# Index scores summed over the heads by TensorE with diagonal weights, instead of by VectorE

## What is computed

```python
sc = jnp.einsum('bqhd,bsd->bqhs', qi, ki)
idx_score = jnp.einsum('bqhs,bqh->bqs', jax.nn.relu(sc), wib)
idx_score = jnp.where(causal[None], idx_score, NEG)
_, sel = lax.top_k(idx_score, k_top)          # k_top = 64
...                                           # softmax attention over the selected keys
```

## Time and profile before

| | |
|---|---|
| median of 3 runs | 1553.19 us (1549.77 to 1553.95) |
| profiled execution | 1555.47 us, of which the span from first to last instruction is 1553.7 us |
| TensorE busy | 1497.1 us, 96% of the span |
| VectorE busy | 1063.1 us, 68% |
| ScalarE busy | 778.6 us, 50% |
| mean granted TensorE clock | 0.990 |

### The profile page before, as it was taken

The page is one execution under the profiler, slowest core; times in us unless marked ns, Lnnn a source line. Parts: engine busy times, 40 slices in busy tenths (PEclk is TensorE's granted clock), DMA queues, the critical chain, the costliest instruction groups (busy, mean ns, idle before and its releaser), DMA issues.

```text
span 1553.7 us, 21682 instructions
## 1 busy us (share of the span) xinstructions
PE 1497.1 (96%) x8433; PEld 1264.5 (81%) x8433; DVE 1063.1 (68%) x1713; ACT 778.6 (50%) x1162; POOL 123.3 (8%) x98
## 2 busy tenths in 40 slices
PE   8989999999899999999999999999999999999997
PEld 5767888888777888878877988888788779888886
DVE  7767588667866787676345566878864455677777
ACT  4564444434464444433655344666545653446563
POOL 0130000000220000011022000000010320000000
PEclk9999999999999999999999999999999999999999
DMA  7624655655334755654614745556536147355551
GB/s 257 199 99 139 201 192 190 211 179 192 117 120 155 242 192 188 219 173 135 190 59 151 252 134 171 185 189 217 175 122 193 53 150 258 125 168 185 189 189 67
DMA packets 184429, 265.03 MB, mean 171 GB/s; under 512 B 7368, under 2 KB 139398, under 8 KB 184200
## 3 DMA queue, kind: packets, MB, share of 16 engines
q1 hardware_dynamic: 178712, 258.38, 50.1%
q10 hardware_dynamic: 5616, 5.26, 1.0%
HBM read 258.38 MB, written 5.24 MB: 170 GB/s over the span
## 4 chain that ended last, share of the span: by engine, by line
PE 77%; DVE 13%; ACT 5%; issue 2%; DVEq 2%; POOL 1%; ACTq 0%; POOLq 0%; DMA 0%; SPq 0%
PE psw L815 18%; PE psw L814 8%; PE psw L742 8%; PE psw L744 7%; PE psw L743 7%; DVE wlo L1736 5%; PE psa L742 4%; PE psa L744 4%; PE psa L743 4%; PE psa L874 3%; PE psa L876 3%; PE psa L927 2%; PE psw L898 2%; ACT sy L1452 1%; PE psa L944 1%
## 5 line engine op out<-in xcount | busy, mean ns | idle before, releaser
L1736 DVE TENSOR_TENSOR wlo<-raw,whi 128x2048 fp32r<-128x2048 f32 (+3 forms) x199 | 449.9, 2266 | 125.0 <-ACT whi L1348 124.5
L815 PE MATMUL psw<-xboth,whi 128*128 128x512 f32 x1344 | 464.8, 396 | 1.2 <-DVE wlo L1736 1.2
L1348 ACT ACTIVATE whi<-raw 128x2048 fp32r<-128x2048 f32 (+3 forms) x199 | 375.2, 1886 | 175.8 <-PE psw L744 91.3
L814 PE MATMUL psw<-xboth,wlo 128*128 128x256 f32 x1176 | 327.9, 279 | 0.0
L815 PEld LDWEIGHTS psw<-xboth,whi 128*128 128x128 f32 x1344 | 242.7, 188 | 49.1 <-DVE wlo L1736 2.3
L814 PEld LDWEIGHTS psw<-xboth,wlo 128*128 128x128 f32 x1176 | 221.7, 189 | 7.5
L742 PE MATMUL psw<-whi,xboth 128*128 128x512 f32 (+3 forms) x472 | 182.1, 386 | 5.3 <-DVE wlo L1736 5.3
L744 PE MATMUL psw<-whi,xboth 128*128 128x512 f32 (+3 forms) x472 | 178.9, 379 | 0.0
L743 PE MATMUL psw<-wlo,xboth 128*128 128x512 f32 (+3 forms) x472 | 178.9, 379 | 0.0
L1410 ACT ACTIVATE r<-psw 128x512 f32<-128x512 f32 x88 | 52.5, 596 | 174.6 <-PE psw L815 164.0
L742 PE MATMUL psa<-whi,rr 128*128 128x512 f32 x352 | 137.5, 391 | 1.4 <-DVE rr L2366 1.4
(11 more groups left out here) (290 smaller groups left out, 2210.1 us busy)
## 6 DMA issues: line engine op xcount, KB each, us to landing
raw<-in_w_gu SPq DMA_DIRECT2D x44, 1024.0 KB, 5.1
raw<-in_ffn_w_up SPq DMA_DIRECT2D x42, 1024.0 KB, 5.1
raw<-in_w_down SPq DMA_DIRECT2D x22, 1024.0 KB, 4.9
raw<-in_ffn_w_down SPq DMA_DIRECT2D x22, 1024.0 KB, 4.9
raw<-in_w_in SPq DMA_DIRECT2D x20, 1024.0 KB, 5.3
raw<-in_xa_wkv SPq DMA_DIRECT2D x16, 1024.0 KB, 5.3
raw<-in_w_o SPq DMA_DIRECT2D x8, 1024.0 KB, 5.1
raw<-in_w_out SPq DMA_DIRECT2D x8, 1024.0 KB, 5.2
```

The costliest lines, as they stand in the source:

```text
L814: pe.matmul(bank[:, 0:S], wl[:, k, cols], xhi[:, k, :], start=False, stop=False)
L815: ins = pe.matmul(bank.rearrange("p (i s) -> p i s", i=2), wh[:, k, cols], xboth[:, :, k, :], start=k == 0, stop=k == KD - 1)
L1348: nc.scalar.activation(tile_flat("hi", i), tile_flat("raw", i), ACT.Copy).then_inc(hi_ready, 1)
L1736: v.tensor_tensor(tile_flat("lo", i), tile_flat("raw", i), tile_flat("hi", i).bitcast(F32), ALU.subtract).then_inc(lo_ready, 1)
```

## The change

For each tile, ScalarE makes eight diagonal matrices `diag` (the identity scaled, row by row, by the query's weight for a head), and TensorE multiplies each with the head's relu'd scores and accumulates the eight products in one PSUM bank (`index_sum`, now TensorE's). VectorE only adds the mask while it copies that sum out (`index_out`). Scores, relu and head transposes move in all three programs, two PSUM banks of late heads change (`head_banks`), and the top-k rounds are spread anew: four of tile 0 ahead of the last rope, two behind it, two in step 0 of attention, and tile 1's eight over steps 1 to 5 as 2, 1, 2, 1 and 2.

```diff
+TOP_STEPS = {0: (0, 6, 8), 1: (1, 0, 2), 2: (1, 2, 3), 3: (1, 3, 5), 4: (1, 5, 6), 5: (1, 6, 8)}
+        diag = cblocks[:, 0:2048].rearrange("p (t h s) -> p t h s", t=NT, h=H)
+        isum_banks = [psw[:, 0, :], psa[:, 2, :]]
+        head_banks = [(psa, 0), (psa, 1), (psw, 2), (psw, 1), (psw, 3), (psa, 0), (psa, 1), (psa, 3)]
...
+                def index_sum(t):                                   # TensorE
+                    nk = (t + 1) * P
+                    pe.wait_ge(relu_done, NT * l + t + 1)
+                    pe.wait_ge(diag_ready, NT * l + t + 1)
+                    for h in range(H):
+                        ins = pe.matmul(isum_banks[t][:, 0:nk], diag[:, t, h, :], relu[:, h, 0:nk],
+                                        start=h == 0, stop=h == H - 1)
+                    ins.then_inc(isum_done, 1)
+                def second_scores():
+                    pe.wait_ge(proj_ready, 8 * l + 5)
+                    index_sum(0)
+                    index_scores(1)
...
-                             (6, 0): first_scores})
-                pe.wait_ge(relu_done, NT * l + 1)
-                index_scores(1)
-                pe.wait_ge(proj_ready, 8 * (l + 1))
-                for q in range(2, 8):
...
+                             (5, 1): first_scores, (6, 0): second_scores})
+                pe.wait_ge(qkb_roped, NT * (l + 1))
+                for q in range(2, 5):
+                    pe.wait_ge(proj_ready, 8 * l + q + 4)
+                    head_turns(q)
+                index_sum(1)
+                for t in range(NT):
+                    pe.wait_ge(qka_roped[t], l + 1)
+                for q in range(5, 8):
                     head_turns(q)
                 pe.wait_ge(heads_ready, 8 * (l + 1))
-                pe.wait_ge(relu_done, NT * (l + 1))
+                pe.wait_ge(icomb_done, NT * (l + 1))
...
+                def diagonals(t):                                   # ScalarE
+                    act.wait_ge(qki_roped, NT * (l + 1))
+                    for h in range(H):
+                        ins = nc.scalar.activation(diag[:, t, h, :], ident[:], ACT.Copy, scale=wi_s[:, t, h:h + 1])
+                    ins.then_inc(diag_ready, 1)
...
-                evict(1, "in", l, 7, 3, proj_out, {(1, 0): second_tokens},
-                      {(2, 1): params_out, (3, 1): memory_out, (4, 1): first_heads_out, (5, 1): lambda: rectified(0)})
-                rectified(1)
+                evict(1, "in", l, 7, 3, proj_out,
+                      {(1, 0): second_tokens, (5, 1): lambda: rectified(0), (6, 0): lambda: rectified(1)},
+                      {(2, 1): params_out, (3, 1): memory_out, (4, 1): first_heads_out, (6, 0): lambda: diagonals(1)})
...
-                def index_sum(t):                                   # VectorE
-                    for h in range(H):
-                        ins = v.scalar_tensor_tensor(out=sc, in0=relu[:, h, 0:nk], scalar=wi_s[:, t, h:h + 1],
-                                                     in1=cm if h == 0 else sc, op0=ALU.mult, op1=ALU.add)
+                def index_out(t):
+                    v.tensor_tensor(iscore[:, t, 0:nk], isum_banks[t][:, 0:nk], causal[:, S - nk:S],
+                                    ALU.add).then_inc(icomb_done, 1)
```

More of the change, by code:

```diff
@@ L403, in build @@
         relu_done = sem("relu_done")
+        diag_ready = sem("diag_ready")
+        isum_done = sem("isum_done")
         icomb_done = sem("icomb_done")
@@ L1027, in head_turns @@
                 def head_turns(q):
+                    bank, place = head_banks[q]
                     for j, b in enumerate(head_groups[q]):
                         for t in range(NT):
-                            ins = pe.transpose((psa if q < 2 else psw)[:, q % 4, j * S + t * P:j * S + (t + 1) * P],
+                            ins = pe.transpose(bank[:, place, j * S + t * P:j * S + (t + 1) * P],
                                                roped[:, t, b * P:(b + 1) * P], ident[:])
@@ L1542, in first_heads_out @@
                     heads_out(1)
+                    diagonals(0)
                 def proj_out(g, t):
@@ L2022, in _, with top_rounds @@
                                             ALU.subtract, ALU.mult).then_inc(x_ready, 1)
-                def index_sum(t):
+                def index_out(t):
                     nk = (t + 1) * P
-                    dve.wait_ge(relu_done, NT * l + t + 1)
-                    sc = iscore[:, t, 0:nk]
-                    cm = causal[:, S - nk:S]
-                    for h in range(H):
-                        ins = v.scalar_tensor_tensor(out=sc, in0=relu[:, h, 0:nk], scalar=wi_s[:, t, h:h + 1],
-                                                     in1=cm if h == 0 else sc, op0=ALU.mult, op1=ALU.add)
-                        if h < H - 1:
-                            dve.drain()
-                    ins.then_inc(icomb_done, 1)
+                    dve.wait_ge(isum_done, NT * l + t + 1)
+                    v.tensor_tensor(iscore[:, t, 0:nk], isum_banks[t][:, 0:nk], causal[:, S - nk:S],
+                                    ALU.add).then_inc(icomb_done, 1)
+                    dve.drain()
+                def top_rounds(t, r0, r1):
+                    nk = (t + 1) * P
+                    sc = iscore[:, t, 0:nk]
+                    for _ in range(r0, r1):
+                        v.max(out=top8[:], in_=sc)
+                        dve.drain()
+                        v.match_replace(out=sc, in_to_replace=top8[:], in_values=sc, imm_value=TAKEN)
+                        dve.drain()
+                    if r1 == TOPK // 8:
+                        v.tensor_scalar(dmask[:, t, 0:nk], sc, TAKEN / 2, MASKED, ALU.is_gt, ALU.mult)
+                        dve.drain()
+                        v.tensor_tensor(dmask[:, t, 0:nk], dmask[:, t, 0:nk], causal[:, S - nk:S], ALU.add)
+                        dve.drain()
                 t1 = sy[:, 0, 0:640]
@@ L2099, in _ @@
                 serve((1, "in", l, 6))
-                index_sum(1)
-                dve.drain()
+                top_rounds(0, 4, 6)
+                index_out(1)
                 def top(step):
-                    if step >= 6:
-                        return
-                    t, part_ = divmod(step, 3)
-                    nk = (t + 1) * P
-                    sc = iscore[:, t, 0:nk]
-                    for _ in range((part_ + 1) * (TOPK // 8) // 3 - part_ * (TOPK // 8) // 3):
-                        v.max(out=top8[:], in_=sc)
-                        dve.drain()
-                        v.match_replace(out=sc, in_to_replace=top8[:], in_values=sc, imm_value=TAKEN)
-                        dve.drain()
-                    if part_ == 2:
-                        v.tensor_scalar(dmask[:, t, 0:nk], sc, TAKEN / 2, MASKED, ALU.is_gt, ALU.mult)
-                        dve.drain()
-                        v.tensor_tensor(dmask[:, t, 0:nk], dmask[:, t, 0:nk], causal[:, S - nk:S], ALU.add)
-                        dve.drain()
+                    if step in TOP_STEPS:
+                        top_rounds(*TOP_STEPS[step])
                 def mask(kind, h, t):
```

14 lines of the change are left out of this document (4 added, 10 removed).

## The result

The changed kernel took 1557.19 us (median of 7 runs, 1556.49 to 1559.64), the kernel before 1553.19 us beside it (median of 7 runs): the ratio is 1.0032, with a 95% interval of 1.0022 to 1.0043. The predicted time was 1557.5. Slower by 0.32% is at the edge of what was called no change, and the interval leaves out a ratio of 1. The profiled execution took 1557.24 us, its span 1555.3, with a mean granted clock of 0.996; the kernel before took 1555.47 us in its profiled execution, at 0.990.

The account below looks back on a forecast made before the run. TensorE, busy nearly all the time, was taken to bound the kernel. Two layers at +2.7 us give +5.4, less 1.1 of clock: +4.3 on the median of 1553.19, so 1557.5 us, range 1553.5 to 1561.0.

Parts of the forecast that it names:

- TensorE's added work: Float32 products of the two sums: 1.9 us for tile 0, 3.66 for tile 1, 5.56 us a layer.
- How much falls into waits: Between input stage and attention, only 1.4 of 5.56 us fill waits; attention begins 4.15 us later a layer.
- Rival D: TensorE's sums hide because VectorE sets the pace behind the input stage: 1546.4 us; chance 0.05.
- ScalarE's diagonals: Copies around the input stage: 0.3 us each, 2.4 for eight; both groups hide, the second's copy with 0.2 to spare.
- Rival C: ScalarE's diagonals hold TensorE up, 1560.1 us, or tile 0's sum costs as 256 columns, 1561.0; chance 0.15.
- Attention: Gives back 0.75 us at the staging wait (3.03 to 2.3) plus 0.7 late in attention, 1.45 a layer.
- The wait of the earlier trace: TensorE's wait of 0.72 us late in layer 0's attention, at 104.25, was to go.
- The sum: Both layers +5.4 us, less 1.1 of clock: +4.3, so 1559.8 against the profiled execution, 1557.5 on the median.
- The clock: Low clock behind the staging wait returns in both layers at 1.7 us each, 1.1 us less than before.
- Rival B: Clock stays up behind the shorter staging wait in one layer or both: 1555.8 or 1554.1 us; chance 0.30.

Follow-up runs that it names:

- e5: The changed kernel with TensorE's eight products for tile 0 issued twice: 1560.33 us, ratio 1.0053.
- e7: e2 with a buffer of its own for tile 0's relu: 1554.64 us, ratio 1.0020.
- e4: The changed kernel with the eight diagonals of tile 1 made twice on ScalarE: 1561.12 us, ratio 1.0052.
- e6: The kernel before with the sixteen diagonals made by ScalarE and used by nothing: 1553.52 us, ratio 1.0008.
- e14: The kernel before once more, word for word, with a second trace: 1553.33 us, ratio 0.9997; its profiled execution took 1550.35 us.
- e1: The changed kernel with tile 0's last two top-k rounds and its mask moved from attention's step 0 to ahead of attention: 1552.8 us, ratio 0.9998.
- e2: The changed kernel with tile 0 summed by VectorE again, without products or diagonals for it: 1558.44 us, ratio 1.0038.

## Why the prediction was right, and where it was off

**TensorE's added work** was put at 5.56 us a layer. It is 1.88 + 3.46 = 5.34. The price of tile 0, from block 2's products, held to 0.02; the 3.66 for tile 1 was the distance between a memory half and the scores behind it and is 0.2 too long. The Trainium skill's page "FP8 and Floating Point Precision" (section "TensorE Precision Notes", four passes for a float32 product) gives 1.71 and 3.41 us, an estimate worked out from it; the measured 3.46 lies nearer to it than to my row, the 1.88 nearer to my row.

**How much falls into waits.** The heads' transposes and the last values of layer 0 in the first trace of before:

```profile
53.29 0.82 PE L1031 MATMUL psa<-ident,r 128*128 128x128 f32 x6
...
120.43 1.09 PE L927 MATMUL psa<-pt,r 128*64 128x128 f32 x16 [0.74 <-ACT pt L1468]
```

From the heads' transposes to the first scores the time grew from 71.94 - 53.29 = 18.65 to 22.41 us: 3.76 later, where 4.15 was said. The 0.4 is the shorter sum and transposes of 1.09 where 1.28 was reckoned. That a sum in the stage can't hide is shown by doubling it (e5, both layers) and by taking it out (e7, in full in layer 0). For the sum of tile 1 it is read from the rows, not from a run of its own. Rival D is excluded.

**ScalarE's diagonals**: 0.29 us from one to the next against 0.3, both groups covered, about 0.5 us of cover behind the second (e4), nothing from the first (e6). Rival C did not occur.

**Attention** gives back 0.54 (layer 0) and 0.80 (layer 1) at the copy of the compressed keys, against 0.75; in layer 0 VectorE stood 0.31 us at issue in the middle of the chain, about the difference between the layers. The wait of the earlier trace rows went, as said: the same products stand at 103.75 without one. In e14 they have no such wait either, but one of 0.71 us two steps sooner. What holds in both traces of before is the stretch from the transposes behind the second memory half to the last values: 33.26 and 33.25 us in layer 0, and 32.46 in the changed kernel, 0.8 less (0.7 in layer 1), where 0.7 was said. e1 shows that the mask and the two rounds between the maxima are all but 0.35 of the remaining 2.49.

**The sum.** From the heads' transposes to the last values the changed kernel takes 119.93 - 53.13 = 66.80 us in layer 0 and 454.35 - 386.06 = 68.29 in layer 1, of which 5.41 - 3.72 = 1.69 is low clock. Against the second trace of before, whose layers hold no low clock that costs anything, the change costs 66.80 - 64.36 = 2.44 and 68.29 - 1.69 - 64.37 = 2.23 us: 4.67 for both, where the prediction had 5.4. The 0.7 us lie ahead of attention, which begins 7.5 us later over both layers and not 8.3; attention gives back 2.9 us, as said.

**The clock** is the step that failed in its working, though the total did not suffer. I took the low clock for a fixed price of that wait, 1.7 us in each layer after the change, and 1.1 less than before. The changed kernel paid it in one layer, not both. And its price before, 2.8 and 1.7 us, belonged to one execution: another one of the same kernel paid none in either layer. The rule of the Trainium skill's page "TensorE: Matmul & The Clock Gate" (section "Why this matters for your kernels", keep the gaps between bursts short) did not decide here: in layer 1 a gap of 3.03 us kept the clock in e14, and one of 2.23 us lost it in the changed kernel. Where the gap went (e1), the low clock went from both layers. Rival B, that the clock stays up, happened in half, in layer 0 of that one execution; behind the same 2.49 us in e5 the clock was down. That the time of 1557.5 fell within 0.4 us of the measured median owes much to luck. On the footing of the profiled executions the forecast was 1559.8, 4.3 us over 1555.47, and 1557.24 was measured, 1.8 us over. Of the 2.5 us between them 0.7 are work that was overestimated and 1.7 the clock, which gave back 2.8 us and not 1.1. The forecast for the median put the same 4.3 us on a median that lies 2.3 us below its profiled execution, while the changed kernel's median lies at its own, and that hides the miss.

**Still open.** Before's runs lie at about 1550.0, 1553.3 and 1555.7 us. The first and the last have a trace; the middle one, where the median lies, has none, and what it consists of is open. The mean granted clock of the runs doesn't settle it: 0.991 to 0.995 at the lowest level, 0.991 to 0.994 at the middle one and 0.990 at the highest, so only the highest stands out by more low clock. Whether the low stretch begins in the wait of layer 0 or 9 us ahead of it differs from one execution to the next, and no run here controls it.

## What to carry to other kernels

Moving work from a half-idle engine to the one that is busy all the time costs the length of that work, minus the waits at its new place. Here 5.3 us a layer went in, the start of attention came 3.8 us later, and 2.2 to 2.4 us a layer remained. The profit is in what the freed engine does with its time. The change left the last two rounds and the mask between two maxima that the bottleneck waits for; put into VectorE's new idle time they give back as much as the whole change had cost.

When an experiment removes work and wins nothing, look first for the buffer that the removed and the remaining step share (e2 and e7). And take two traces before a clock stretch gets a price: the same low clock can lie in a wait that hides it. A difference that is read from one trace must not be put on a median of other executions without looking at how far the two lie apart.

## What the runs showed of the hardware

- A ScalarE copy of 128 columns of float32 with its scale through a pointer lasts 0.39 us; in a row of eight (2.44 us) each starts 0.29 us behind the one before.
- Eight float32 products of 128x128 weights take 1.88 us with 128 columns and 3.46 us with 256.
- The low clock does not follow from the length of a single wait. Waits of 3.03 us (e14, layer 1) and 2.49 us (changed kernel, layer 0) left it up. Waits of 3.03 (before, both layers), 2.49 (e5, layer 0) and 2.23 us (changed kernel, layer 1) ended in it.
- The same kernel has several levels of time, 1550.0, 1553.3 and 1555.7 us. In the two traces the highest and the lowest differ by 5.1 us, of which 67.14 - 64.36 + 66.06 - 64.37 = 4.5 us are stretches of low clock in the two layers that the change touches.
